# The experts' sum in a hybrid attention and retrieval block: VectorE makes every second low part, from eight tiles ahead

## What is computed

```python
def peer_layer(x, w_q, keys1, keys2, u_tab, v_tab):
    ...
    eidx = jnp.take_along_axis(cidx, pos, axis=-1)
    gate = jax.nn.softmax(sc, axis=-1).astype(x.dtype)
    def one_block(args):
        xb, eb, gb = args
        u = jnp.take(u_tab, eb, axis=0)
        a = jnp.einsum('nhkd,nd->nhk', u, xb)
        w = jax.nn.gelu(a, approximate=False) * gb
        vv = jnp.take(v_tab, eb, axis=0)
        return jnp.einsum('nhk,nhkd->nd', w, vv)
```

## Time and profile before

| | |
|---|---|
| runs, us | 1447.18, 1447.79, 1447.69 |
| profiled execution, us | 1447.31 |
| its span, us | 1445.6 |
| TensorE busy | 99% |
| VectorE busy | 73% |
| GpSimd busy | 70% |
| ScalarE busy | 42% |
| TensorE's granted clock | 0.998 of full (2.4 GHz) |

### The profile page before, as it was taken

One profiled execution on the slowest core, in us unless ns is written; L12 is line 12 of the kernel. 1 busy time (PEld: TensorE's weight loads), 2 busy tenths in 40 slices (PEclk: granted clock), 3 DMA queues, 4 the chain that ended last, 5 costly groups with the idle time before them and its releaser, 6 DMA issues.

```text
span 1445.6 us, 24823 instructions
## 1 busy us (share of the span) xinstructions
PE 1424.1 (99%) x8029; PEld 1266.3 (88%) x8029; DVE 1051.2 (73%) x2206; ACT 607.4 (42%) x1018; POOL 1011.6 (70%) x629
## 2 busy tenths in 40 slices
PE   9999999999999999999999999999999999999997
PEld 5888778889999999999999999878888888888885
DVE  5466666688999999899986694867555555555587
ACT  5666741334333354444444443333333333333333
POOL 3432331335598878887887689889888888888885
PEclk9999999999999999999999999999999999999999
DMA  6212120423599979999999899999999999999981
GB/s 241 74 59 103 59 89 4 144 86 126 171 351 320 298 265 378 393 420 405 391 364 386 321 397 387 344 371 368 355 362 359 356 356 343 351 356 339 359 336 71
DMA packets 136909, 406.97 MB, mean 282 GB/s; under 512 B 13905, under 2 KB 56657, under 8 KB 134673
## 3 DMA queue, kind: packets, MB, share of 16 engines
q1 hardware_dynamic: 80384, 240.67, 46.6%
q0 software_dynamic: 39760, 142.76, 25.1%
q10 hardware_dynamic: 16704, 22.81, 4.3%
HBM read 355.50 MB, written 50.14 MB: 281 GB/s over the span
## 4 chain that ended last, share of the span: by engine, by line
PE 82%; DVE 5%; POOL 4%; issue 4%; DMA 2%; ACT 2%; SPq 0%; ACTq 0%; POOLq 0%; DVEq 0%
PE banks L1831 13%; PE banks L1833 13%; PE banks L1832 13%; PE banks L1886 12%; PE banks L1888 11%; PE banks L1887 11%; POOL lo L457 3%; PE banks L1948 2%; POOL rows L765 2%; PE banks L2104 1%; PE banks L2105 1%; DMA raw<-v_tab 1%; PE banks L2041 1%; PE banks L1932 1%; DVE rows L1365 1%
## 5 line engine op out<-in xcount | busy, mean ns | idle before, releaser
L457 POOL TENSOR_TENSOR lo<-raw,hi 128x1024 fp32r<-128x1024 f32 x290 | 700.5, 2417 | 344.0 <-ACT hi L451 328.0
L1831 PE MATMUL banks<-x1T_hi,hi 128*128 128x368 f32 (+3 forms) x1168 | 395.3, 338 | 0.3 <-DVE x1T_lo L1337 0.3
L1832 PE MATMUL banks<-x1T_lo,hi 128*128 128x368 f32 (+3 forms) x1168 | 390.0, 334 | 0.0
L1833 PE MATMUL banks<-x1T_hi,lo 128*128 128x368 f32 (+3 forms) x1168 | 389.9, 334 | 0.0
L451 ACT ACTIVATE hi<-raw 128x1024 fp32r<-128x1024 f32 x291 | 305.8, 1051 | 22.4 <-DMA raw<-v_tab 13.0
L1886 PE MATMUL banks<-hi,wgt_hi 128*128 128x512 f32 x750 | 292.0, 389 | 1.7 <-DVE wgt_lo L1703 1.7
L1887 PE MATMUL banks<-lo,wgt_hi 128*128 128x512 f32 x750 | 291.8, 389 | 0.0
L1888 PE MATMUL banks<-hi,wgt_lo 128*128 128x512 f32 x750 | 291.8, 389 | 0.0
L1703 DVE TENSOR_TENSOR wgt_lo<-wgt,wgt_hi 128x384 fp32r<-128x384 f32 x125 | 101.0, 809 | 185.8 <-ACT wgt_hi L1118 185.5
L1831 PEld LDWEIGHTS banks<-x1T_hi,hi 128*128 128x128 f32 x1168 | 219.3, 188 | 4.8 <-DVE x1T_lo L1337 0.6
L1833 PEld LDWEIGHTS banks<-x1T_hi,lo 128*128 128x128 f32 x1168 | 219.1, 188 | 4.4
(11 more groups left out here) (240 smaller groups left out, 1753.4 us busy)
## 6 DMA issues: line engine op xcount, KB each, us to landing
raw<-u_t SPq DMA_DIRECT2D x128, 512.0 KB, 5.9
raw<-v_tab SPq DMA_DIRECT2D x128, 512.0 KB, 6.8
g_scratch<-stage SPq DMA_DIRECT2D x12, 2048.0 KB, 11.7
gelu_scratch<-gelu ACTq DMA_DIRECT2D x116, 192.0 KB
ga<-gelu_scratch SPq DMA_DIRECT2D x29, 768.0 KB, 7.7
gg<-g_scratch SPq DMA_DIRECT2D x14, 1536.0 KB, 11.5
raw<-w SPq DMA_DIRECT2D x26, 512.0 KB, 3.4
raw<-w_pq SPq DMA_DIRECT2D x16, 512.0 KB, 3.6
```

What stands on the lines that cost most here:

```text
L457: eng.tensor_tensor(l[:, :], raw[:, c % RAW_SLOTS, :], h[:, :].bitcast(F32), ALU.subtract).then_inc(lo_ready, 1)
L1831: pe.matmul(o, h[:, s], hiT[:, k, tokens], start=(k == 0), stop=False)
L1832: pe.matmul(o, h[:, s], loT[:, k, tokens], start=False, stop=False)
L1833: ins = pe.matmul(o, l[:, s], hiT[:, k, tokens], start=False, stop=(k == KT - 1))
```

## The change

A constant `SHARED_FROM` stands for the eighth tile ahead of the V tiles, U 120. From there on every odd tile's low part is made by VectorE and counted by a semaphore of its own, `odd_lo_ready`; the even ones stay with GpSimd and `lo_ready`. All who wait for a low part (the loads, TensorE in both stages) wait for the semaphore of that tile. VectorE makes U 121, 123, 125 and 127 behind the dots 7, 9, 11 and 15 of the last 16, V 1 before it waits for the gelu of the last U tile, and from V tile 2 on the low part of V tile k + 1 between `add_row(k)` and `weight_lo(k)`, for each even k. GpSimd goes through the V tiles in steps of two: it waits for two slots of rows, makes one low part and issues two gathers. No token changes its way, and the arithmetic is the same.

```diff
+SPLIT_AFTER = {7: 1, 9: 3, 11: 5, 15: 7}
...
-VECTOR_TILES = 2
+SHARED_FROM = S_V - 8
...
+        def by_vector(c):
+            return c > SHARED_FROM and c % 2 == 1
+
+        def wait_lo(eng, c, it):
+            if isinstance(it, int):
+                c, it = c + 4 * it, 0
+            if by_vector(c):
+                wait(eng, odd_lo_ready, 2 * it + (c - SHARED_FROM + 1) // 2)
+            elif c >= SHARED_FROM:
+                wait(eng, lo_ready, 2 * it + (SHARED_FROM + (c - SHARED_FROM) // 2 + 1))
+            else:
+                wait(eng, lo_ready, 4 * it + (c + 1))
...
-            eng.tensor_tensor(l[:, :], raw[:, c % RAW_SLOTS, :], h[:, :].bitcast(F32), ALU.subtract).then_inc(lo_ready, 1)
+            eng.tensor_tensor(l[:, :], raw[:, c % RAW_SLOTS, :], h[:, :].bitcast(F32),
+                              ALU.subtract).then_inc(odd_lo_ready if by_vector(c) else lo_ready, 1)
...
-                if not split_first:
+                if not split_first and not by_vector(tile[0]):
                     split_lo(pool, *tile)
...
             def v_octet(first, o):
-                for k in range(8):
-                    gather(v_rows, [U_ROWS + first * ROWS + k + AHEAD], o, (S_V + 8 * first + k, 2 * o))
+                for k in range(0, 8, 2):
+                    at = U_ROWS + first * ROWS + k + AHEAD
+                    gather(v_rows, [at, at + 1], o, (S_V + 8 * first + k, 2 * o))
...
-            for c in range(N_TILES - 8, N_TILES - VECTOR_TILES):
+            for c in range(N_TILES - 8, N_TILES, 2):
                 split_lo(pool, c, 0)
...
                     dot(k, r)
+                    if (n := ROWS * (r - R_PRE - R_MID) + k) in SPLIT_AFTER:
+                        split_lo(dve, SHARED_FROM + SPLIT_AFTER[n], 0)
...
+            split_lo(dve, S_V + 1, 0)
             dve.wait_ge(gelu_ready, ETILES)
...
                     add_row(k, i)
+                    if k % 2 == 0 and (k or split == 0):
+                        split_lo(dve, S_V + 8 * par + k + 1, 4 * j)
                     if k >= split:
                         weight_lo(k, 2 * i)
...
+                if k % 2 == 0:
+                    split_lo(dve, S_V + k + 1, 0)
                 if NO_ROWS - 1 <= k < ETILES - 1:
                     tile_weights(k + 1)
                 weight_lo(k, 0)
-                c = S_V + k + 1
-                if c >= N_TILES - VECTOR_TILES and c < N_TILES:
-
-                    dve.wait_ge(lo_ready, c)
-                    split_lo(dve, c, 0)
```

More of the change, by code:

```diff
@@ L294, in build @@
         lo_ready = sem("lo_ready")
+        odd_lo_ready = sem("odd_lo_ready")
         tile_used = sem("tile_used")
@@ L434, in weight_parts @@
             return wgt_hi[k % 2], wgt_lo[k % 2]
+        def by_vector(c):
[9 more added lines that the diff above has]
+                wait(eng, lo_ready, 4 * it + (c + 1))
         def load_tile(eng, c, it, src):
-            wait(eng, lo_ready, 4 * it + (c - RAW_SLOTS + 1))
+            if not (isinstance(it, int) and c + 4 * it < RAW_SLOTS):
+                wait_lo(eng, c - RAW_SLOTS, it)
             eng.dma_start(raw[:, c % RAW_SLOTS, :], src).then_inc(raw_loaded[c % RAW_SLOTS], 16)
@@ L739, in gather @@
                 even = r if isinstance(r, int) else 0
-                if split_first and tile is not None:
+                if split_first:
                     split_lo(pool, *tile)
@@ L1822, in features @@
                 if part == 0:
-                    pe.wait_ge(lo_ready, 4 * it + (c + 1))
+                    wait_lo(pe, c, it)
                 h, l = parts_of(c)
@@ L2157, in parts_there @@
             def parts_there(k, it):
-                pe.wait_ge(lo_ready, 4 * it + (S_V + k + 1))
+                wait_lo(pe, S_V + k, it)
                 pe.wait_ge(wgt_lo_ready, 4 * it + (k + 1))
```

## The result

The changed kernel takes 1449.43 us (median of 20 runs, 1448.31 to 1451.5); beside them the kernel before took 1445.73 (20 runs, 1445.15 to 1447.79). The ratio is 1.0024, with a 95% interval of 1.0018 to 1.0031: slower by 0.24% (0.18 to 0.31), 3.5 us. The ratio is not that of the two medians, which lie 3.7 apart. Forecast was 1448.9 and "no change, a hair slower": the time lies in the range, but the step up is three times the +1.2 of the sum. The larger part of that is that the kernel before is faster than the three runs known when the forecast was made; the rest is mainly that the waits at the end of the U tiles were sized too small. Ratios leave out one execution of a later experiment, e10, which took 2382.83 at a granted clock of 0.556.

The account below looks back on a forecast made before the run. TensorE, busy 1424.1 of 1445.6 us, bounds the kernel. 0.96 − 1.10 + 1.1 + 0.2 = +1.2 on the profiled 1447.31 gives 1448.5, against the median 1448.9; range 1446.0 to 1451.4.

Parts of the forecast that it names:

- V tile 2, +0.96: Before V tile 2, wgt_lo comes later because VectorE's and GpSimd's subtractions exclude each other: +0.96 us, lower end −0.91.
- the second way that the step named: At V tile 2, VectorE goes first and GpSimd's 2.40 lies between its two subtractions; same end within 0.1 us.
- V tile 15, −1.10: Before V tile 15, the gap closes as GpSimd's low part of V 12 starts 1.4 us sooner: −1.10 us, ends −1.10 and 0.
- The end of the U tiles, +1.1: Before U 127, a row gather issued about 7 us sooner delays V 0's load: +1.1 us, ends 0 and 2.3.
- The other cause: End of the U tiles: V 0's load queues behind U 127's, which waits for U 123's late low part; upper end 2.5 us.
- The end, +0.2: Last eight tiles: VectorE makes four low parts instead of two, and GpSimd may hold the ports: +0.2 us, ends 0 and 0.6.
- The settled part, 0: Settled V tiles: VectorE's low part takes 1.22 of 1.83 us free in every second tile, leaving 0.6; cost 0.
- gathers in pairs, 0: Paired gathers, the new semaphore and waits of two rows at once cost 0, as rows are asked for four tiles ahead.
- Both gaps close and nothing opens: Rival: the waits before V 2 and V 15 both go, V 0's load is no later; 1445.7 us, chance 13%.
- V 16 stays late: Rival: V 16's load stays late with DMA engines full, so the V 15 gap remains; +1.10, 1450.0 us, chance 12%.
- VectorE becomes the late one: Rival: VectorE's low part ahead of wgt_lo delays TensorE; two places from 922 to 972 give 1452.5 us, chance 13%.
- The forecast's own range: 1447.2 to 1450.6 us around 1448.9, said to follow from the ends of the terms; forecast's chance 62%.

Follow-up runs that it names:

- e10: Kernel before, no low part moved, with the third and fourth gathers of expert rows issued early: 1451.02 us, ratio 1.0031.
- e8: Kernel before, unchanged, run and profiled a second time: median 1445.87 us, ratio 1.0004.
- e1: Changed kernel with the low parts of the U tiles back on GpSimd, V tiles still shared: 1446.95 us, ratio 1.0005.
- e4: Changed kernel with the first four gathers of expert rows held until the low part of U 127 is made: 1446.87 us, ratio 1.0004.
- e13: Changed kernel, unchanged, run and profiled a second time: 1449.21 us, ratio 1.0021 to the kernel before.
- e2: Changed kernel with only the U tiles' low parts moved to VectorE, V tiles as in the kernel before: 1448.23 us, ratio 1.0013.
- e3: Changed kernel with VectorE making wgt_lo of V 2 ahead of the low part of V 3: 1447.98 us, ratio 1.0015.

## Why the prediction was right or wrong, point by point

- **The base.** Here is the larger error. The sum started from an execution of 1447.31 whose 2.01 of waits I took for the kernel's. e8 has none of them and takes 1444.95; the three runs known then (1447.18 to 1447.79) are the three slowest of the 20. So "V tile 15: −1.10" was right against that profile and worth nothing against a run without the late load, and of the 0.91 at V 2 too such a run has nothing. From 1444.95 the sum would be +0.91 +0.96 (V 2) +1.1 (U tiles) +0.2 = 1448.1; measured 1449.43. Forecast and result lie 0.5 apart because base and step were off in opposite directions, and that is luck. Beside e8, the waits of the changed kernel are 3.79 and 0.13 at the end, 3.92, where the sum had 1.16; of the 2.76 between them, 2.01 are waits that stood in the base, 0.88 is the U tiles' term, and V 2 and the end make −0.06 and −0.07.
- **V tile 2, +0.96**: 0.90 measured (1.81 − 0.91), and 1.77 to 1.82 lost in four profiles with this order. It went the second way that the step named: VectorE came first and GpSimd's subtraction lay between its two, with the same end. The full block of the Trainium skill (SBUF — State Buffer, Who interferes with whom) is borne out at this place in e1 (GpSimd's 2.40 became 3.40) and e4 (VectorE's 1.22 became 3.36) too; shared ports would have given −0.91. One reading goes too far: that at both places of the kernel before the one that issues second is blocked. At the first, VectorE's start on record is the earlier one (916.16, GpSimd's 916.24), and VectorE is blocked; the rows show the block there, not who issued second.
- **V tile 15, −1.10**: no wait there in either profile of the changed kernel. But the reason given (an earlier low part of V 12) is not shown to be the cause, since the unchanged kernel lacks the wait too in e8.
- **The end of the U tiles, +1.1**: 1.98 in one profile, 2.42 in the other. The cause chosen, gathers going out sooner ahead of V 0's load, is shown by e4. The size failed twice. One gather of 512 KB was counted, 1.3, as leaving about 7 sooner; it left 4.8 sooner (897.96, not 902.74), but all four went sooner, and V 0's load took 2.3 longer (13.2 against 10.9). And the gates, loaded just ahead of V 0, were not in the step at all: they came so late that `wgt` began 2.36 later, and with it the gelu of U 124, which stands behind `wgt_hi`: 902.20, not 900.27. That gave a wait of its own before U 126. The other cause, the sync queue standing behind the low part of U 123, did not occur in the first profile (VectorE came first at 885.89, and V 0's load left at 893.43, as before, 893.53). It did in e13, as the prediction reckoned it (ready at 889.0), and moved the high part of V 0 by 0.32: the choice against it was right.
- **The end, +0.2**: 0.13, in the last tiles, right in kind and near in size. **The settled part, 0**, and **gathers in pairs, 0**: right; 0.73 was left where 0.6 was reckoned. The early gathers of rows do not come from the pairs: e2, without pairs, has them (890.25 to 897.05) and the wait; e1, with pairs, has neither. They come from the low parts that GpSimd no longer makes.
- **The rivals.** "Both gaps close and nothing opens" fell: two opened. "V 16 stays late" fell in both profiles; the stretch moved 387 GB/s. The Trainium skill (SBUF — State Buffer, Summary: rules for kernel authors) gives about 358 for transfers from HBM, and the trace again does not agree. "VectorE becomes the late one" did not happen from 922 to 972; its mechanism, a low part ahead of `wgt_lo` with the ports held, is the one at V 2, and e3 shows it at V 4 for 0.75.
- **Chances.** 82% lay on "within 0.2%" and 15% on slower. By the ratio the result is on the other side of that line by 0.04%, its interval across it; in microseconds it is inside (under 1450.6), because that line was drawn from 1447.69. The forecast's own range is said to follow from the ends of its terms, but 1450.6 is the 0.2% line; the upper ends add up to some 1451.5. What should have moved the chances is that three runs within 0.6 us of each other were not a picture of how the kernel before spreads.

## What to carry to other kernels

Before crediting a change with a wait that it removes, see the wait in a second execution of the old kernel: one that ends on a late load may be gone there, and then the change has nothing to win. When work is taken off an engine that also issues transfers, list what that engine will now issue sooner and what then shares the DMA engines with it; holding four gathers back by a few us took away 2.0 us of waits here (e4), with no arithmetic moved. And a two-operand step that TensorE is waiting for belongs ahead of any longer one on VectorE and ahead of the moment GpSimd takes the ports.

## What was not expected of the hardware

- VectorE and GpSimd block each other both ways, by the whole instruction: GpSimd's 2.40 became 3.09 to 3.40 where VectorE was first, VectorE's 0.55 became 2.73 where GpSimd was. Which of the two holds the ports can't be read from starts that lie close: VectorE's is 0.06 earlier in e1 and it goes first (916.10, 916.16), 0.08 earlier in the earlier trace rows and 0.21 earlier in e10 (900.56, 900.77), and there it is blocked. Two GpSimd subtractions in a row left VectorE's waiting multiplication no turn between them: 4.71 (e10).
- The same load took 8.2, 10.9 and 13.2 us from issue to landing (e4, before, after), with the DMA engines full each time (the two queues' shares add up to 1.08 to 1.11 from 894 to 901). Between e4 and after, the gathers' queue makes the difference. The time of issue counts too: in e8 the load left 2.1 sooner than in before and took 11.9, landing 1.1 sooner; in e13 it left 2.25 later than in after and took about 11.2.
- After e10's 2.96 without a matmul TensorE ran at a granted clock of 0.50, its 1.2 GHz level, for the 3 us shown below (U tile matmuls 0.31 apart instead of 0.167), and was back at 1.00 (2.4 GHz) from 911. The waits of 0.7 to 1.8 in the changed kernel left the clock at 1.00.

```profile
907.00:910.00 3.00, 3.00 (x10) 3.00 (x11) 1.20 (x4) 2.32 (x3) 1.32 (x1) 0.50 1.01 410
```
